# Half an output product one step later, and the kept rows and remainders of a norm tile two steps later, at the end of a hybrid decoder layer's second attention

## What is computed

```python
h = rms_norm(x, ln1_g)
o_a = mla_mixer(...)                  # 8 heads, causal softmax
o_b = nsa_mixer(...)                  # 8 heads; gated sum of a compressed, a selected and a window branch
mix = concat([rms_norm(o_a, g_mla), rms_norm(o_b, g_nsa)])
x = x + mix @ w_o
h2 = rms_norm(x, ln2_g)
x = x + square(relu(h2 @ w_up)) @ w_down
```

## Time and profile before

| | us |
|---|---|
| median of 3 runs | 637.51 (637.24 to 637.59) |
| the profiled execution | 635.6 |
| its span, first to last instruction | 633.7 |
| lies around the span | 1.9 |

### The profile page before, as it was taken

How to read it: one execution, slowest core, us unless ns; L and a number is a source line. 1 busy time by engine, 2 the same in 40 slices (tenths; PEclk the granted TensorE clock), 3 DMA queues, 4 the chain that set the end, 5 groups by cost and what they waited for, 6 DMA issues and landing times.

```text
span 633.7 us, 11664 instructions
## 1 busy us (share of the span) xinstructions
PE 624.3 (99%) x4105; PEld 554.0 (87%) x4105; DVE 501.2 (79%) x936; ACT 399.5 (63%) x798; POOL 161.5 (25%) x230
## 2 busy tenths in 40 slices
PE   8999999999999999999999999999999999999998
PEld 7999788887689888887899999999998788888886
DVE  5767765589887878897897777777778999997665
ACT  6675674677897637656458665676647465745551
POOL 0656654434412202112210101111111212222200
PEclk9999999999999999999999999999999999999999
DMA  8883539998989955996355778788877889999984
GB/s 297 317 320 133 199 129 328 284 289 211 261 255 269 359 182 169 286 259 151 67 134 184 220 206 221 200 218 227 186 170 169 235 221 247 228 243 278 239 247 153
DMA packets 35225, 142.48 MB, mean 225 GB/s; under 512 B 5367, under 2 KB 6263, under 8 KB 34208
## 3 DMA queue, kind: packets, MB, share of 16 engines
q1 hardware_dynamic: 23408, 83.79, 37.8%
q0 software_dynamic: 10208, 34.88, 30.1%
q10 hardware_dynamic: 1552, 23.08, 9.6%
HBM read 139.57 MB, written 65.06 MB: 323 GB/s over the span
## 4 chain that ended last, share of the span: by engine, by line
PE 89%; DVE 5%; ACT 2%; issue 2%; DMA 1%; POOL 0%; SPq 0%; ACTq 0%; DVEq 0%; POOLq 0%
PE bank L2151 15%; PE bank L2153 15%; PE bank L2152 15%; PE bank L2555 7%; PE bank L2554 7%; PE bank L2553 7%; PE bank L2171 7%; PE bank L2392 3%; PE bank L2335 2%; PE bank L2374 2%; PE bank L2346 1%; PE bank L2347 1%; PE bank L2428 1%; PE bank L2489 1%; PE bank L2491 1%
## 5 line engine op out<-in xcount | busy, mean ns | idle before, releaser
L882 POOL DMA_DIRECT2D down_sums<-w_down x64 | 50.0, 781 | 228.9 <-PE bank L2555 136.9
L2151 PE MATMUL bank<-w_hi,act_hi 128*128 128x512 f32 (+3 forms) x222 | 88.3, 398 | 1.0 <-DVE act_lo L1441 0.6
L2153 PE MATMUL bank<-w_hi,act_lo 128*128 128x512 f32 (+3 forms) x222 | 79.0, 356 | 0.0
L2152 PE MATMUL bank<-w_lo,act_hi 128*128 128x512 f32 (+3 forms) x222 | 79.0, 356 | 0.0
L1421 DVE TENSOR_TENSOR w_lo<-raw,w_hi 128x1024 fp32r<-128x1024 f32 (+1 forms) x50 | 59.9, 1209 | 19.2 <-ACT w_hi L992 19.0
L1133 ACT ACTIVATE p_buf<-s_buf,stats 128x128 f32<-128x128 f32 (+3 forms) x96 | 53.8, 561 | 31.7 <-PE bank L2171 16.1
L992 ACT ACTIVATE w_hi<-raw 128x1024 fp32r<-128x1024 f32 (+1 forms) x50 | 51.4, 1039 | 32.6 <-DMA raw<-w_pairs 25.1
L1371 ACT ACTIVATE w_hi<-raw 128x1024 fp32r<-128x1024 f32 x31 | 32.8, 1057 | 37.3 <-DMA raw<-down_sums 19.5
L2151 PE MATMUL bank<-w_hi,s_all 128*128 128x512 f32 x140 | 54.6, 390 | 0.0
L2152 PE MATMUL bank<-w_lo,s_all 128*128 128x512 f32 x140 | 54.5, 389 | 0.0
L2153 PE MATMUL bank<-w_hi,s_all 128*128 128x512 f32 x140 | 54.5, 389 | 0.0
(11 more groups left out here) (326 smaller groups left out, 1844.6 us busy)
## 6 DMA issues: line engine op xcount, KB each, us to landing
down_sums<-w_down ACTq DMA_DIRECT2D x32, 512.0 KB, 5.7
down_sums<-w_down POOLq DMA_DIRECT2D x64, 256.0 KB, 5.8
raw<-down_sums SPq DMA_DIRECT2D x32, 512.0 KB, 5.7
up_sums<-w_pairs POOLq DMA_DIRECT2D x28, 512.0 KB, 9.4
raw<-up_sums SPq DMA_DIRECT2D x28, 512.0 KB, 4.8
raw<-weights SPq DMA_DIRECT2D x26, 512.0 KB, 5.6
up_sums<-w_pairs SPq DMA_DIRECT2D x16, 512.0 KB, 6.2
raw<-w_down SPq DMA_DIRECT2D x16, 512.0 KB, 5.3
```

The lines of the kernel that those rows point to most:

```text
L882: pool.dma_start(sums_dram[k, rows_], a["w_down"][SUMS[m][1], step, rows_], accum_op=ALU.add, max_dma_last_dim=4096).then_inc(*sum_added[k ...
L2151: pe.matmul(dst, a_h, w_h, start=start, stop=False, skip_group_check=onto)
L2152: pe.matmul(dst, a_h, w_l, start=False, stop=False, skip_group_check=onto)
L2153: return pe.matmul(dst, a_l, w_h, start=False, stop=stop, skip_group_check=onto)
```

## The change

The second half of the product (1, 2, 1) moves from step 56 to step 57. The two kept halves of tile 2 move from steps 66 and 67 to steps 67 and 69, and with them their remainders, from DVE's steps 67 and 68 to 68 and 70. Nothing is added or removed, and no DMA is issued by what moves.

```diff
-WO_UNITS = [..., 51, 52, 55, 56, 63, 64, 68, 69]
+WO_UNITS = [..., 51, 52, 55, 57, 63, 64, 68, 69]
...
 LN2_AT = {3: (50, 54, 57), 2: (59, 62, 65)}
-KEEP_AT = {3: (58, 60), 2: (66, 67)}
+KEEP_AT = {3: (58, 60), 2: (67, 69)}
```

More of the change, by code:

```diff
@@ L182 @@
 WO_JOBS = [(0, t, c) for c in range(2) for t in range(NT)] + [(1, t, c) for t in reversed(range(NT)) for c in range(2)]
-WO_UNITS = [21, 22, 24, 25, 26, 27, 28, 30, 31, 32, 33, 34, 35, 37, 38, 39, 43, 44, 46, 47, 51, 52, 55, 56, 63, 64, 68, 69]
+WO_UNITS = [21, 22, 24, 25, 26, 27, 28, 30, 31, 32, 33, 34, 35, 37, 38, 39, 43, 44, 46, 47, 51, 52, 55, 57, 63, 64, 68, 69]
 WO_AT = {}
```

## The result

The change made the kernel slower: **639.01 us** (638.35 to 640.65, 7 runs) against 637.27 (635.94 to 637.59, 7 runs) for the kernel before. The medians are 1.74 us apart. The ratio on record is 1.0035, with an interval of 1.0023 to 1.0047 (1.5 to 3.0 us); it is not the quotient of the two medians, which is 1.0027. The forecast was 640.6, slower, with a range of 638.8 to 641.6.

The account below looks back on a forecast made before the run. PE was taken to bound the kernel, busy 99% of the span, with ACT's queue binding one stretch. 1.8 + 1.3 = 3.1 us on the median of 637.51 gave 640.6 us, range 638.8 to 641.6.

Parts of the forecast that it names:

- Edit 1: Half of product (1, 2, 1) moved from step 56 to 57: next exponential on ACT 1.75 us later, taken as 1.8.
- without the bank: Step 57: if the second D bank came free in time for the norm's last four transposes, 1.3 us later remains.
- a stalled PE restarts a little slower: Step 57: reason for taking 1.8 us instead of the 1.75 worked out from the rows.
- Edit 2: Kept rows and remainders of tile 2 moved later: PE starts the `w_up` products 1.29 us later, taken as 1.3.
- The cancelled relief: Compressed product's 0.43 us wait goes, but product (1, 1, 1) waits for the first remainder: 0.1 us later in all.
- the late remainder: Second remainder, behind the addition in DVE's step 70, makes PE start `w_up` at 306.65 instead of 305.36 us.
- The norm of tile 1 stayed covered: Its rows would end at 309.8 us, before PE comes to their transposes at 311.1.
- only one wait binds: Rival: only one of the two waits, in step 57 or ahead of step 74, costs: 638.8 or 639.4 us; chance 0.15.
- No change: Rival: later waits absorb the loss and the time stays within 1.3 us of 637.5; chance 0.06.
- The clock rival: Rival: PE's clock falls to 1.2 GHz behind the new gaps, `w_up` matmuls take 4.4 us more: 645 us; chance 0.04.
- The faster rival: Rival: ACT's queue is relieved, unit 57's exponential starts 0.96 us earlier and the 0.43 wait goes: 636.1 us; chance 0.05.
- its own case: Both delays paid in full, with their bounds 1.4 to 2.1 and 0.9 to 1.5 us: 639.8 to 641.1; chance 0.70.

Follow-up runs that it names:

- edit 2 alone: Only the kept rows and remainders of tile 2 moved, half product left in step 56, against the kernel before: 637.67 us, ratio 1.0014.

## Why the prediction was right

**What bounds the kernel.** A delay that reaches the first `w_up` products was to be kept to the end. It was: 3.05 us at the first squared relu, 3.07 at the last addition, and PE busy for 174.00 of 174.00 us from 326 to 500 us.

**Edit 1, 1.8 us.** The exponential of unit 57 was forecast 1.75 later than 288.11. It came 289.53 - 288.11 = 1.42 later in an execution that was 0.32 early, so 1.74; alone the edit moved the end of the stretch by 1.75. Each link is in the trace: the product of unit 53 started 0.05 after the copy's end, the half product 0.31 behind (forecast 0.33), the first four transposes 1.47 behind that (1.46), the addition 1.67 behind the product's start (1.65), the second four transposes with a wait of their own. The split holds too: the forecast left 1.3 of it without the bank, and 1.40 go when PE's order is put back. The step "a stalled PE restarts a little slower", for which 1.8 was taken, was not needed.

**Edit 2, 1.3 us.** It measured 1.35 alone. The cancelled relief was forecast at 0.1 and is 0.12 where it is isolated; the late remainder is the other 1.23. The forecast put the price on the addition's 0.61 us and the remainder behind it. Both rows are there, and the order on DVE makes the price, as the run with the two swapped shows. The norm of tile 1 stayed covered, as worked out: the transposes began 312.49 - 311.19 = 1.30 after its rows were scaled.

**The rivals.** That only one wait binds falls with the two edits run alone: each costs its own price. No change, that is less than 1.3 us or 0.2%, falls with both timings, 1.0023 and 1.0028 at the least. The clock rival falls by the profile: the granted clock is 1.00 in each stretch above, the one with the gap of 1.06 us and the one with 0.99 among them, that is 2.4 GHz in all of them. The matmuls behind the gaps also take what they took before (128x512 0.39 to 0.40 us, 128x256 0.28). By the rule of the Trainium skill (TensorE: Matmul & The Clock Gate, Part 1: The HAM clock gate) that idleness brings half rate back, a price was possible; the trace agrees only in part: these two gaps, with PE at work on both sides, brought none, while longer ones at the start of other executions were followed by half rate (last section). That gaps as short as these would be enough was the forecast's own assumption for its 645, and not the page's word. And the trace of before could have said something on it: it has a gap of 0.56 us, ahead of the matmul at 11.16 us, in a stretch at 1.00.

The faster rival fell at the point that was named, the order on ACT. DVE had the scores of unit 57 ready at 285.97 (285.69 + 0.28 in the first timeline above). Their exponential started at 289.53, and in between ACT stood idle for 1.12 and for 0.41 us, since two conversions were ahead of it. The Trainium skill (TensorE: Matmul & The Clock Gate, Part 1: The HAM clock gate) says of ACT and DVE that they take their instructions strictly in order; the trace agrees.

**The size, and what was luck.** By the traces the forecast of 3.1 us is right to 0.05. The median of 639.01 is another matter: it lies below the 639.8 to 641.1 that the forecast gave for its own case, and only 0.2 us above the lower end of the range, which reached down that far for the sake of the rival with one wait. So that this median lies in the range is in part luck; the mechanism is borne out by the traces and not by it. In that first set of 7 runs against 7 the medians are 1.74 us apart, 1.3 less than the traces. In the eight comparisons behind it they agree with the traces within 0.5 us, to either side (3.03 for 3.06 and 1.41 for 1.75 longer, for instance, or 1.37 for 0.92 shorter). The scatter at the start of an execution (last section) can do as much; that it accounts for all of it isn't shown. The intervals of the ratios hold the traces' difference in seven of the nine comparisons and miss it by 0.1 us or less in the first and the last. Also, the median on which 3.1 was added, 637.51, belongs to 3 runs; with four more it was 637.27, and two other sets of before gave 636.21 and 636.34. The step that was too simple is the last one, a median of before plus a difference of traces: its base alone moves by over 1 us.

## What to carry to other kernels

Before moving work of a saturated engine to another place in its queue, ask which wait it stands ahead of: here work ahead of a wait was free as far as the wait was long, and moved behind it cost the idle time that it uncovered, 0.67 us of price for 0.66 of wait. A remainder that is made a step ahead of its need is no spare slack: further down its queue it may land behind an instruction that waits for the very engine that needs the remainder, as the addition here did. And where an edit's price is a microsecond, compare traces between two fixed instructions around the edit, and use whole executions only to confirm the sign.

## What was not expected

**The start of an execution scatters by as much as the change costs, and gaps on PE were followed by a lower clock there.** The addition of step 43, ahead of all edits, started between 257.75 and 260.59 us in the ten profiled executions. It is decided within the first 62 us: the same instruction of DVE (L1564) started at 59.18 us in the changed kernel and at 61.85 in the kernel with edit 2 alone, and from there to the addition it is 198.57 and 198.55 us. What happened in the latter, in the timeline of PE and ACT:

```profile
8.65 0.63 ACT L1019 ACTIVATE act_hi<-x_first 128x512 fp32r<-128x512 f32 x1 [2.98 <-DMA x_first<-x_t]
...
10.06 0.45 PE L2151 MATMUL bank<-w_hi,act_hi 128*128 128x384 f32 x1 [2.31 <-DVE act_lo L1441]
...
11.24 0.34 PE L2151 MATMUL bank<-w_hi,act_hi 128*128 128x384 f32 x1
...
12.02 0.52 PE L2151 MATMUL bank<-w_hi,act_hi 128*128 128x384 f32 x1
```

and its stretch from 10 to 15 us (the columns as above):

```profile
10.00:15.00 5.00, 4.94 (x19) 4.94 (x20) 4.58 (x9) 4.67 (x10) 0.00 (x0) 0.66 1.03 408
```

A piece of x landed late, so that ACT's rounding of it began at 8.65; in the trace of before it began at 6.82. PE stood still for 2.31 us, went on at full clock, and some 1.3 us later its matmuls took 0.52 instead of 0.34 us until 14.6 us: a granted clock of 0.66 on the mean of the stretch, so part of it at 1.2 GHz. The kernel with DVE's kept copies had the same (a wait of 2.01 us, then 0.66). The kernel with DVE's order swapped had a wait of 2.25 us at that place and kept 1.00. So what the clock rival supposes was seen in this kernel, behind gaps twice as long as those of the change, and not each time. The forecast's remark that no stretch of before shows the lower level also needs a caveat: in that trace, too, 128x384 matmuls took 0.52 us at the start of PE's work (from 5.77 to 6.73 us), though the clock is listed as 1.00 there. The durations say more than the listed clock in that place. Which piece of x is late in which execution was not tried; nothing in the edits touches it.

**The same copy is dearer on DVE and still pays there.** The kept copy of 128x512 takes 0.59 us on ACT and 0.69 on DVE, but moving two of them took 0.96 from a queue without idle time and left a wait of 0.30 on PE. The kernel as a whole gained 0.67 by it.
